# Seven quadrant products for the last six K blocks of the down projection

## The chip, the cores and the metric

The kernel runs on one core of one Trainium2 chip. The metric is the device time of one execution in microseconds (us). Its engines are PE (matrix multiplication), DVE (VectorE), ACT (ScalarE), POOL (GpSimd) and SP (SyncE, which issues the transfers here). Each engine works through its own list of instructions in order and waits on semaphores for the others.

## The reference

One layer of a streaming encoder over 544 tokens (512 of a prompt, 32 of a sample) and 1024 columns, in float32. The change concerns its last steps alone:

```
x = x + mo
x = x + swiglu(rmsnorm(x), w_gate, w_up, w_down)   # (silu(xn @ w_gate) * (xn @ w_up)) @ w_down
y = rmsnorm(x) * norm_final                        # after the only layer
```

w_gate and w_up are 1024 x 2816, w_down is 2816 x 1024: its K dimension has 22 blocks of 128 rows, its output 8 blocks of 128 columns.

## The kernel before

**Exact products.** Each float32 operand is split into a high part and a low part (ACT writes the high part, a cast to float32r; DVE writes the rest, a subtraction). One product of a 128 x 128 weight block with 272 tokens then is three matmuls: high x high, high x low, low x high. The 544 tokens are two halves of 272.

**Units of seven products.** Most of the work is cut into 2 x 2 quadrants (two output blocks, two groups of K blocks) and done by a Strassen scheme: seven products take the place of eight. In one unit PE runs `seven(q, s)`: products f = 0 to 6, each over KQ = 4 K blocks, 12 matmuls each, 84 in all. The weights of a unit come in one transfer of 1 MB into one of the two slots of `w_raw`. DVE makes three rows of sums of the quadrants (`w_sums`, line 1750 and 1754), ACT casts raw quadrants and sums into `w_hi` (its `form`, line 1124), DVE subtracts into `w_lo` (its `form`, line 1764). While PE runs unit q, ACT and DVE make the forms of unit q + 1. `form` 5 reads the last raw quadrants of a slot; SP starts the next transfer into that slot when DVE has finished it. On the way ACT copies four partial results out of PSUM (`copy_part`, line 1135, after f = 0, 1, 2 and 4), and PE waits for the copies of f = 0, 1, 2 and 4 before f = 2, 3, 4 and 6.

**The order of the feed-forward units.** `FFN` lists 30 units n = 0 to 29 in three groups c = 0, 1, 2 of 4, 4 and 3 pairs (`PAIRS`): a gate unit and an up unit for each pair of hidden blocks, and after the first gate unit of c = 1 and of c = 2 four down units, which take the eight hidden blocks of the group before. For these, each pair of hidden blocks is split in seven forms (`h_first`, `h_second`, `h_sums`, `h_sum2`, `h_sum4` on ACT, their `low_` counterparts on DVE); this happens beside the next gate unit. In c = 2 the pairs are only split plainly (`h_high` on ACT, `h_low` on DVE, line 2064).

**The tail.** The last six K blocks (NF2) of w_down belong to c = 2 and are done plainly, one output block at a time (phase "down", `unit`, `product_half`): 8 blocks x 2 halves x 6 K blocks x 3 = 288 matmuls, the last block in parts of 256 and 288 tokens. After each block DVE adds it to `resid` in `x_last`, ACT squares it (`y_sq`), POOL sums the squares (`y_sum`), PE transposes the block of the time before (`turn_y`, five transposes) and DVE writes it times `norm_final` to `y_tok`. The last block is followed by the norm of its tokens in two parts (`last_sums`, `last_norm`), the scaling of `y_tok` and six stores.

Of the kernel before, what the change touches and what calls it, by code (L numbers as in the profile page):

```python
# [39 lines left out]
    "down": (4, 2, 1),  # L40
# [106 lines left out]
def trunk_kernel(nc, x_t, cols, w_in, w_quads, ln_g, ln_b, w_s, b_s, w_pa, w_pb, w_o, w_gate, w_up, w_down_quads, w_down, norm_final,  # L147
# [30 lines left out]
    with ctx:  # L178
# [31 lines left out]
        cols64, _ = sb("cols64", [P, 9 * KD])  # L210
# [89 lines left out]
        hf_lo, _ = sb("hf_lo", [P, HFORMS, KQ, HALF], F32R, at=lo_at)  # L300
        h_quads = up_sb[:].rearrange("p i (h n) -> p (i h) n", h=2)
# [107 lines left out]
        h_ready = sem("h_ready")  # L409
# [7 lines left out]
        rstd_ready = sem("rstd_ready")  # L417
        y_turned = sem("y_turned")
        y_in_tok = sem("y_in_tok")
        ysq_done = sem("ysq_done")  # L420
# [17 lines left out]

        def form_source(q, f, slot):

            kind, n, _, _ = PRODUCTS[f]
            src = w_raw[:, slot, :].rearrange("p (f n) -> p f n", f=4) if kind == "raw" else w_sums
# [10 lines left out]
        def first_free(q):  # L453

            if q < QG:
                return firsts_taken, q + 1
            kind, c, m = FFN[q - QG]
            if kind == "down":
                return firsts_taken, QG + KQ * c + m + 1
            return (gate_made if kind == "gate" else h_made), 2 * (KQ * c + m) + 2  # L460

# [7 lines left out]
        def _(sp):  # L469
# [31 lines left out]
            def load_down(p, j, s, row, blocks, q=None):  # L501
                if q is None:
                    slot_free(p, j, s)
                else:
                    sp.wait_ge(raw_loaded[s % 2], 16)
                    sp.wait_ge(form_lo, NGROUP * q + FORM_AT[5])
                dst = w_raw[:, s % 2, 0:blocks * P].rearrange("p (k n) -> p k n", k=blocks)
                src = row_blocks(w_down, slice(row, row + blocks * P), 2 * j + s, P)
                sp.dma_start(dst, src).then_inc(raw_loaded[s % 2], 16)
# [93 lines left out]
            for n in range(len(FFN)):  # L603
                load_ffn(ph["ffn"], n)
            for s in range(2):
                load_down(ph["down"], 0, s, 0, NF2, q=QE - 2 + s)
            load_down(ph["down"], 1, 0, 0, NF2)
            sp.wait_ge(form_used, NPROD * QE)
            sp.dma_start(gf_all[:], norm_final.rearrange("(a d) -> a d", a=1).to_broadcast((P, D))).then_inc(gf_loaded, 16)
            load_down(ph["down"], 1, 1, 0, NF2)  # L610
            with sp.Fori(2, 4) as j:
                for s in range(2):
                    load_down(ph["down"], j, s, 0, NF2)
# [22 lines left out]
        def _(pe):  # L636
# [202 lines left out]
            def product(q, s, f, blocks, forms, there=None):  # L839
# [3 lines left out]
                for k in blocks:  # L843
# [6 lines left out]
                    last = pe.matmul(out, wlo, xhi, start=False, stop=k == KQ - 1, skip_group_check=not opens)  # L850
                last.then_inc(form_used, 1)

            def seven(q, s, first=None, behind={}, bank_b=None, forms=x_forms, h_made=None):
# [4 lines left out]
                def h_there(x, k):  # L858

                    if k == KQ - 1:  # L860
                        pe.wait_ge(hf_ready, h_made + {A11: 2, A12: 2, A22: 2, S3: 3, S1: 3, S2: 4, S4: 5}[x])

                for f in range(NPROD):
# [18 lines left out]
                    product(q, s, f, range(KQ), forms, there if first is not None else h_there if h_made is not None else None)  # L882
# [49 lines left out]
            seven(QG + 1, 1, behind={2: lambda: spread(r_diag, diag_ready, CH + 1, r_turned)}, bank_b=p.taken[1])  # L932
            for n, (kind, c, m) in enumerate(FFN):
                if n >= 2:
                    seven(QG + n, n % 2, behind={2: lambda: spread(r_diag, root_diag, CH + 1, root_turned)} if n == 4 else {},
                          forms=h_forms if kind == "down" else x_forms,
                          h_made=5 * (KQ * c + KQ - 1) if kind == "down" and m == 0 else None)

            def down_ready(k, h):
                if h == 0:  # L940
                    pe.wait_ge(h_ready, 2 * (k // 2) + 2)

            p = ph["down"]

            def down(j, s, ready=None):
                unit(p, j, s, H0, NF2, ready=ready)

            def turn_y(j, s):

                pe.wait_ge(dve_out[s], p.out_before(j, s) + 2)  # L950
                turn_tokens(ps_misc[s], x_last[:, s, :]).then_inc(y_turned, 1)

            pe.wait_ge(*first_free(QE - 2))
            pe.wait_ge(lo_ready, p.unit(0, 0))
            pair_free(p, 0, 0, 0)
            for h in range(2):
                product_half(p, 0, 0, 0, h, NF2, H0, P, down_ready, range(NF2 - 2), closes=False)
            for h in range(2):
                product_half(p, 0, 0, 0, h, NF2, H0, P, down_ready, (NF2 - 2, NF2 - 1), opens=False)
            pe.wait_ge(quad_out, 2 * QE)  # L960
            pe.wait_ge(*first_free(QE - 1))
            with pe.Fori(0, 3) as j:
                down(j, 1)
                turn_y(j, 0)
                down(j + 1, 0)
                turn_y(j, 1)
            pe.wait_ge(lo_ready, p.unit(3, 1))
            pair_free(p, 3, 1, 0)

            def last_block(part, behind):  # L970

                tokens, out = LAST[part], ps_main[:, 1, part, 0:LAST[part].stop - LAST[part].start]
                for k in range(NF2):
                    whi, wlo = w_hi[:, 1, k * P:(k + 1) * P], w_lo[:, 1, k * P:(k + 1) * P]
                    xhi, xlo = act_hi[:, H0 + k, tokens], act_lo[:, H0 + k, tokens]
                    pe.matmul(out, whi, xhi, start=(k == 0), stop=False)
                    pe.matmul(out, whi, xlo, start=False, stop=False)
                    last = pe.matmul(out, wlo, xhi, start=False, stop=(k == NF2 - 1))
                    if k in behind:
                        behind[k]()  # L980
                last.then_inc(tile_half, 1)

            def turn_last(part):

                pe.wait_ge(dve_out[1], p.out_before(3, 1) + part + 1)
                for c in LAST_CHUNKS[part]:
                    dst = ps_g[0:P, 0, c * P:(c + 1) * P] if c < CH else ps_g[0:NS, 1, 0:P]
                    last = pe.transpose(dst, x_last[:, 1, c * P:c * P + ROWS[c]], ident[:, :])
# [19 lines left out]
            last_block(0, {0: lambda: turn_y(3, 0)})  # L1008
            last_block(1, {0: rest_of_sums, 1: lambda: turn_last(0), 2: lambda: last_sums(0)})
# [4 lines left out]
        def _(act):  # L1014
# [104 lines left out]
            def form(q, s, f):  # L1119
# [4 lines left out]
                act.copy(f_hi[:, form_group(q, f), :], form_source(q, f, s)).then_inc(third_hi if f == 3 else form_hi, 1)  # L1124
# [195 lines left out]
            def h_high(j, i, n):  # L1320

                act.wait_ge(h_made, NF1 + n)
                act.copy(act_hi[:, H0 + 2 * j + i, :], up_sb[:, i, :]).then_inc(h_hi, 1)

# [30 lines left out]
            def h_first(n, m):  # L1355
                act.wait_ge(h_made, 2 * n + 2)
                act.copy(hf_hi[:, A11, m, :], up_sb[:, 0, 0:HALF]).then_inc(hf_split, 1)
# [13 lines left out]
            def down_hi(p):  # L1371

                act.wait_ge(raw_loaded[0], 16 * p.loads(0, 0))
                act.copy(w_hi[:, 0, 0:NF2 * P], w_raw[:, 0, 0:NF2 * P]).then_inc(hi_ready, 1)

            def up_free(n, f):
# [5 lines left out]
                elif kind == "down" and m == 0 and f == 2:  # L1382
                    act.wait_ge(hf_ready, 5 * KQ * (c + 1))
# [4 lines left out]
                elif kind == "up" and m and c < 2 and f == 2:  # L1388
                    act.wait_ge(hf_ready, 5 * pair)
                elif kind == "up" and m and c == 2:  # L1390
                    act.wait_ge(h_ready, 2 * m)

            def beside(n):
# [5 lines left out]
                if n == 1:  # L1399
                    return {3: lambda: silu(1, 1), 5: lambda: silu(2, 0)}  # L1400
                if kind == "up":
                    return {1: lambda: silu(2 * pair + 1, 1), 3: lambda: silu(2 * pair + 2, 0)}
                if kind == "down":
                    return {}
                if c == 2 and m:
                    return {0: lambda: h_high(m - 1, 1, 2 * m - 1), 2: lambda: h_high(m - 1, 0, 2 * m)}
# [7 lines left out]
            def seven(n, others):  # L1414
# [4 lines left out]
                for f in range(NPROD):  # L1419
# [1059 lines left out]
```

## Time and profile before

| | |
|---|---|
| three runs | 850.44, 850.85, 850.92 us; median 850.85 |
| profiled execution | 849.98 us, of which the span of the trace is 848.1 us |
| PE busy | 838.3 us, 99% of the span |
| DVE busy | 698.3 us, 82% |
| ACT busy | 448.3 us, 53% |
| granted clock of PE | 0.996 over the span |

An engine that is busy for 99% of the span sets the time; the others matter where PE would wait for them. The trace counts from the span's start.

### The profile page before, as it was taken

What the parts mean: (1) busy time and instruction counts of PE and PEld (TensorE: products, weight loads), DVE (VectorE), ACT (ScalarE), POOL (GpSimd) and SP (SyncE); (2) the same over time, 40 slices, a digit from 0 to 9 for tenths busy, and PEclk for the clock granted to TensorE, in tenths of its full rate; (3) what the DMA queues carried; (4) which work ended last, traced back from release to release, by engine and by line L of the source; (5) the groups of instructions that cost most, each with busy time, mean ns of one, the idle gap of its engine ahead of it and who ended that gap; (6) DMA issues with size and microseconds to landing.
All of it is one profiled execution on the core that took longest, in us unless ns stands there. A gap on an engine that the chain in (4) does not pass through costs nothing.

```text
span 848.1 us, 16289 instructions
## 1 busy us (share of the span) xinstructions
PE 838.3 (99%) x6654; PEld 836.6 (99%) x6654; DVE 698.3 (82%) x1094; ACT 448.3 (53%) x764; POOL 17.7 (2%) x23
## 2 busy tenths in 40 slices
PE   9999999999999999999999999999999999999996
PEld 9999999999999999999999999999999999999995
DVE  6868878789898989845568899999999999888554
ACT  8432225556565656652245786665566665466422
POOL 0000000000000000000000000000000000000031
PEclk9999999999999999999999999999999999999998
DMA  9333314132323232241542122222222232232222
GB/s 306 111 101 103 106 51 152 50 104 96 104 97 103 98 104 98 99 149 51 168 137 100 51 100 100 101 100 100 101 100 100 101 100 100 100 100 70 92 63 106
DMA packets 39495, 88.49 MB, mean 104 GB/s; under 512 B 2176, under 2 KB 28800, under 8 KB 33024
## 3 DMA queue, kind: packets, MB, share of 16 engines
q1 hardware_dynamic: 39424, 87.49, 30.6%
q8 instruction: 52, 0.85, 0.4%
q14 instruction: 19, 0.16, 0.1%
HBM read 85.10 MB, written 2.38 MB: 103 GB/s over the span
## 4 chain that ended last, share of the span: by engine, by line
PE 99%; DVE 0%; POOL 0%; issue 0%; DVEq 0%; ACT 0%; POOLq 0%
PE ps_main L848 13%; PE ps_main L849 13%; PE ps_main L850 13%; PE ps_main L653 10%; PE ps_main L651 10%; PE ps_main L652 10%; PE ps_t L848 7%; PE ps_t L849 7%; PE ps_t L850 7%; PE ps_g L794 1%; PE ps_g L696 1%; PE ps_t L678 1%; PE ps_main L708 0%; PE ps_main L707 0%; PE ps_main L706 0%; PE ps_g L678 0%
## 5 line engine op out<-in xcount | busy, mean ns | idle before, releaser
L848 PE MATMUL ps_main<-xf_hi,w_hi 128*128 128x272 f32 x756 | 218.6, 289 | 0.0
L849 PE MATMUL ps_main<-xf_lo,w_hi 128*128 128x272 f32 x756 | 218.5, 289 | 0.0
L850 PE MATMUL ps_main<-xf_hi,w_lo 128*128 128x272 f32 x756 | 218.4, 289 | 0.0
L651 PE MATMUL ps_main<-act_hi,w_hi 128*128 128x272 f32 x692 | 201.0, 290 | 0.0
L653 PE MATMUL ps_main<-act_hi,w_lo 128*128 128x272 f32 x692 | 200.0, 289 | 0.0
L652 PE MATMUL ps_main<-act_lo,w_hi 128*128 128x272 f32 x692 | 199.1, 288 | 0.0
L1764 DVE TENSOR_TENSOR w_lo<-w_sums,w_hi 128x1024 fp32r<-128x1024 f32 x150 | 129.8, 865 | 25.3 <-ACT w_hi L1124 24.5
L848 PEld LDWEIGHTS ps_main<-xf_hi,w_hi 128*128 128x128 f32 x756 | 142.4, 188 | 0.0
L850 PEld LDWEIGHTS ps_main<-xf_hi,w_lo 128*128 128x128 f32 x756 | 142.3, 188 | 0.0
L849 PEld LDWEIGHTS ps_main<-xf_lo,w_hi 128*128 128x128 f32 x756 | 142.2, 188 | 0.0
L1124 ACT CAST w_hi<-w_sums 128x1024 fp32r<-128x1024 f32 x150 | 114.0, 761 | 51.2 <-DVE w_sums L1754 30.4
L651 PEld LDWEIGHTS ps_main<-act_hi,w_hi 128*128 128x128 f32 x692 | 130.3, 188 | 0.2
L652 PEld LDWEIGHTS ps_main<-act_lo,w_hi 128*128 128x128 f32 x692 | 130.4, 188 | 0.0
L653 PEld LDWEIGHTS ps_main<-act_hi,w_lo 128*128 128x128 f32 x692 | 130.1, 188 | 0.0
L848 PE MATMUL ps_t<-xf_hi,w_hi 128*128 128x272 f32 x420 | 121.5, 289 | 0.0
L849 PE MATMUL ps_t<-xf_lo,w_hi 128*128 128x272 f32 x420 | 121.4, 289 | 0.0
L850 PE MATMUL ps_t<-xf_hi,w_lo 128*128 128x272 f32 x420 | 121.3, 289 | 0.0
L1764 DVE TENSOR_TENSOR w_lo<-w_raw,w_hi 128x512 fp32r<-128x512 f32 (+1 forms) x102 | 95.6, 938 | 5.1 <-ACT w_hi L1124 4.8
L1124 ACT CAST w_hi<-w_raw 128x512 fp32r<-128x512 f32 (+1 forms) x102 | 83.6, 819 | 16.9 <-PE ps_t L850 10.8
L848 PEld LDWEIGHTS ps_t<-xf_hi,w_hi 128*128 128x128 f32 x420 | 79.1, 188 | 0.2
L850 PEld LDWEIGHTS ps_t<-xf_hi,w_lo 128*128 128x128 f32 x420 | 79.0, 188 | 0.0
L849 PEld LDWEIGHTS ps_t<-xf_lo,w_hi 128*128 128x128 f32 x420 | 79.0, 188 | 0.0
(279 smaller groups left out, 1285.9 us busy)
## 6 DMA issues: line engine op xcount, KB each, us to landing
w_raw<-in_w_quads_dram SPq DMA_DIRECT2D x20, 1024.0 KB, 4.8
w_raw<-in_w_gate_dram SPq DMA_DIRECT2D x11, 1024.0 KB, 4.9
w_raw<-in_w_up_dram SPq DMA_DIRECT2D x11, 1024.0 KB, 4.8
w_raw<-in_w_down_quads_dram SPq DMA_DIRECT2D x8, 1024.0 KB, 4.9
w_raw<-in_w_in_dram SPq DMA_DIRECT2D x6, 1024.0 KB, 5.1
w_raw<-in_w_pa_dram SPq DMA_DIRECT2D x4, 1024.0 KB, 5.8
w_raw<-in_w_pb_dram SPq DMA_DIRECT2D x4, 1024.0 KB, 5.2
w_raw<-in_w_o_dram SPq DMA_DIRECT2D x4, 1024.0 KB, 6.8
```

Of the source, the lines that this page charges most:

```text
L651: pe.matmul(out, whi, xhi, start=(opens and k == order[0]), stop=False)
L652: pe.matmul(out, whi, xlo, start=False, stop=False)
L653: last = pe.matmul(out, wlo, xhi, start=False, stop=(closes and k == order[-1]))
L678: last = pe.transpose(dst, src[:, c * P:c * P + ROWS[c]], ident[:, :])
L696: pe.matmul(ps_g[:, 1, 0:P], ones[:, :], ones[:, :], start=True, stop=True)
L794: pe.matmul(ps_g[:, 0, c * P:(c + 1) * P], tok[:, c, group], ws_t[:, g, :], start=True, stop=True)
L848: pe.matmul(out, whi, xhi, start=opens and k == 0, stop=False, skip_group_check=not opens)
L849: pe.matmul(out, whi, xlo, start=False, stop=False, skip_group_check=not opens)
L850: last = pe.matmul(out, wlo, xhi, start=False, stop=k == KQ - 1, skip_group_check=not opens)
L1124: act.copy(f_hi[:, form_group(q, f), :], form_source(q, f, s)).then_inc(third_hi if f == 3 else form_hi, 1)
L1764: dve.tensor_tensor(f_lo[:, group, :], form_source(q, f, s), fbits(f_hi[:, group, :]), ALU.subtract).then_inc(third_lo if f == 3 else form ...
```

## The change

The tail becomes three more units of seven products, n = 30, 31 and 32 in `FFN`, each over KE = 3 K blocks a side (63 matmuls), for output blocks 0 to 5. The forms of a pair of c = 2 are made as for the other groups, with `h_first` and its low part over both halves (544 columns). Output blocks 6 and 7 stay plain column blocks of 36 matmuls ("tiles" 0 and 1): tile 0 runs ahead of unit 30, tile 1 after unit 32. Their weights (384 KB) come into slot 1 of `w_raw` by transfers of their own, `load_tile`. The norm follows the order of blocks 6, 1, 0, 3, 2, 5, 4, 7. For the blocks of places 5 and 6 of that order (5 and 4) ACT scales by `norm_final` ahead of the transposes (`y_scale`) and copies the transposed block to `y_tok` (`y_rows`).

```diff
-    return tuple(order)
+    return tuple(order + [("down", len(PAIRS) - 1, m) for m in range(3)])
...
+            def load_tile(q, t):
+
+                sp.wait_ge(raw_loaded[1], 16)
+                sp.wait_ge(form_lo, NGROUP * q + FORM_AT[5])
+                dst = tile_blocks(1).rearrange("p (k n) -> p k n", k=NF2)
+                sp.dma_start(dst, row_blocks(w_down, slice(0, NF2 * P), t, P)).then_inc(raw_loaded[1], 16)
...
+            load_end(first_end)
+            load_tile(ENDS - 1, KD - 2)
+            load_end(first_end + 1)
+            sp.wait_ge(form_used, NPROD * ENDS)
             sp.dma_start(gf_all[:], norm_final.rearrange("(a d) -> a d", a=1).to_broadcast((P, D))).then_inc(gf_loaded, 16)
...
+            load_end(first_end + 2)
+            load_tile(QE - 2, KD - 1)
...
+            def tile_ahead():
+
+                pe.wait_ge(tile_split, 1)
+                for h in range(2):
+                    tile_half_products(0, ps_g[:, h, 0:HALF], h, range(NF2 - 2), closes=False)
+                for h in range(2):
+                    tile_half_products(0, ps_g[:, h, 0:HALF], h, (NF2 - 1, NF2 - 2), opens=False)
...
+            turns = {ENDS - QG: {3: lambda: turn_y(0)}, ENDS - QG + 1: {5: lambda: turn_y(1)},
+                     ENDS - QG + 2: {2: lambda: turn_y(2), 4: lambda: turn_y(3), 5: lambda: turn_y(4)}}
...
+            pe.wait_ge(tile_split, 2)
+            tile_half_products(1, ps_main[:, 1, 0, 0:HALF], 0, range(NF2), behind={1: lambda: turn_y(5)})
+            pe.wait_ge(quad_out, 2 * QE)
+            tile_half_products(1, ps_main[:, 1, 1, 0:HALF], 1, range(NF2),
+                               behind={0: rest_of_rows, 2: lambda: turn_last(0), 3: lambda: last_sums(0)})
...
+            def tile_high(t):
+
+                act.wait_ge(raw_loaded[1], 16 * (raw_count(ENDS + 1) - 1 + 2 * t))
+                act.copy(tile_hi[t], tile_form(t, tile_hi[t])).then_inc(tile_cast, 1)
...
+                if kind == "up" and pair == NPAIR - 1:
+                    return {0: lambda: tile_high(0), 1: lambda: silu(2 * pair + 1, 1), 3: lambda: silu(2 * pair + 2, 0),
+                            5: lambda: h_second(pair, m)}
...
+                    return ({2: load_root, 4: lambda: y_squares(0)}, {0: lambda: y_squares(1), 5: lambda: y_squares(2)},
+                            {0: lambda: tile_high(1), 1: lambda: y_squares(3), 3: lambda: y_squares(4),
+                             6: lambda: end_block(5)})[m]
...
+                if q == ENDS + 1:
+                    take_y(0)
+                elif q == ENDS + 2:
+                    tile_low(1)
+                    take_y(2)
```

The first place is ACT during unit 29, the last up unit. `ps_t` is the bank whose copy follows f = 0, `part_112` that of f = 1; the cast of `w_raw` is form 0 of the next unit. Before:

```order
L1135 ACTIVATE ps_t<-ps_t 128x272 [waits form_used]
L1135 ACTIVATE part_112<-ps_main 128x272 [waits form_used,h_ready]
L1318 ACTIVATE gate_sb<-gate_sb 128x544 [waits gate_made]
L1135 ACTIVATE up_sb<-ps_t 128x272 [waits form_used,h_ready]
L1374 CAST w_hi<-w_raw 128x768 [waits raw_loaded0]
```

There the cast of a tail block came behind the copy of f = 2. With the change, between the copies of f = 0 and f = 1, now stands form 0 of unit 30, and behind it the cast of tile 0 (`hf_hi` holds it), which waits for the transfer into slot 1:

```order
L1190 ACTIVATE ps_t<-ps_t 128x272 [waits form_used]
L1179 CAST w_hi<-w_raw 128x384 [waits raw_loaded0]
L1427 CAST hf_hi<-w_raw 128x3x256 [waits raw_loaded1]
L1190 ACTIVATE part_112<-ps_main 128x272 [waits form_used]
L1373 ACTIVATE gate_sb<-gate_sb 128x544 [waits gate_made]
```

So the cast of a tail block moved ahead of the copy of f = 1, and form 0 of a further unit ahead of it.

The second place is ACT at the end of unit 32, from the copy of f = 4 on; before the change, a block was transposed straight from the `x_last` that DVE writes. With the change ACT stands between the end of a unit and the transposes of blocks 5 and 4 (`x_last` is now ACT's):

```order
L1190 ACTIVATE parts_103<-ps_main 128x272 [waits form_used]
L1435 ACTIVATE y_sq<-resid 128x544 [waits parts_taken,ysum_done,form_used]
L1440 ACTIVATE x_last<-resid,cols_61 128x544
L1435 ACTIVATE y_sq<-resid 128x544 [waits ysum_done,firsts_taken]
L1440 ACTIVATE x_last<-resid,cols_61 128x544
```

Two scalings and two squares moved here, behind the wait for all of unit 32.

On PE the transposes of block 5 stand behind six matmuls of tile 1, and wait for that scaling:

```order
L1003 MATMUL ps_main<-hf_hi,w_hi 128x272 [waits tile_split]
L1004 MATMUL ps_main<-hf_lo,w_hi 128x272
L1005 MATMUL ps_main<-hf_hi,w_lo 128x272
L1003 MATMUL ps_main<-hf_hi,w_hi 128x272
L1004 MATMUL ps_main<-hf_lo,w_hi 128x272
L1005 MATMUL ps_main<-hf_hi,w_lo 128x272
L722 MATMUL ps_g<-ident,x_last 128x128 [waits y_in_tok,y_scaled]
```

Before, the transposes behind such a block waited for DVE's `x_last` of the block before it (`dve_out0`, `dve_out1`).

## Rows read from the trace of the kernel before

**Rows 1.** The page, parts 1 and 2: busy us and share of the span, granted clock.
```profile
PE 838.3 (99%) x6654; PEld 836.6 (99%) x6654; DVE 698.3 (82%) x1094; ACT 448.3 (53%) x764; POOL 17.7 (2%) x23
PEclk9999999999999999999999999999999999999998
```

**Rows 2.** Busy time by stretch: PE, weight loads, DVE, ACT, POOL, clock, DMA.
```profile
760.00:770.00 10.00, 10.00 (x82) 10.00 (x81) 8.99 (x14) 5.88 (x12) 0.00 (x0) 1.00 0.28 88
```

**Rows 3.** Timeline of ACT, start and duration: copies of f = 0, then tail casts.
```profile
777.20 0.38 ACT L1135 ACTIVATE ps_main<-ps_main 128x272 f32<-128x272 f32 x1 [0.89 <-PE ps_main L850]
787.80 0.38 ACT L1135 ACTIVATE ps_t<-ps_t 128x272 f32<-128x272 f32 x1 [0.89 <-PE ps_t L850]
789.37 0.40 ACT L1135 ACTIVATE part<-ps_main 128x272 f32<-128x272 f32 x1 [1.19 <-PE ps_main L850]
...
826.26 0.83 ACT L1452 CAST w_hi<-w_raw 128x768 fp32r<-128x768 f32 x1 [3.69 <-PE ps_main L653]
827.00 0.65 ACT L1460 ACTIVATE y_sq<-x_last 128x544 f32<-128x544 f32 x1
```

**Rows 4.** Timeline around the start of unit 19, after a gate unit with all forms.
```profile
681.97 0.38 ACT L1135 ACTIVATE ps_t<-ps_t 128x272 f32<-128x272 f32 x1 [0.57 <-PE ps_t L850]
682.14 1.22 DVE L1764 TENSOR_TENSOR w_lo<-w_raw,w_hi 128x1024 fp32r<-128x1024 f32 x1
683.43 0.33 SPq L493 DMA_DIRECT2D w_raw<-in_w_down_quads_dram  x1
```

**Rows 5.** Timeline of DVE in that gate unit, 18.
```profile
675.33 0.69 DVE L1754 TENSOR_TENSOR w_sums<-w_sums,w_raw 128x512 f32<-128x512 f32 x1
675.94 0.44 DVE L2081 SCALAR_TENSOR_TENSOR up_sb<-gate_sb,up_sb 128x272 f32<-128x272 f32 x1
676.29 0.44 DVE L2104 TENSOR_TENSOR hf_lo<-up_sb,hf_hi 128x272 fp32r<-128x272 f32 x1
...
679.08 0.73 DVE L2111 TENSOR_TENSOR hf_lo<-gate_sb,hf_hi 128x544 fp32r<-128x544 f32 x1
679.71 0.45 DVE L1779 TENSOR_TENSOR gate_sb<-parts 128x272 f32<-128x272 f32 x1
```

**Rows 6.** SP's load into slot 1 in the same place of unit 29.
```profile
787.49 0.38 SPq L509 DMA_DIRECT2D w_raw<-in_w_down_dram  x1
```

**Rows 7.** Line 509, the loads of 384 KB: all eight, to landing.
```profile
DMA to landing us min/median/max: 3.1/3.4/3.4
```

**Rows 8.** Timeline of the tail: one transposed block, and the next.
```profile
805.74 0.71 PE L678 MATMUL ps_t<-ident,x_last 128*128 128x128 f32 x5
810.82 0.71 PE L678 MATMUL ps_g<-ident,x_last 128*128 128x128 f32 x5
...
832.01 0.69 DVE L2289 TENSOR_TENSOR y_tok<-ps_g,gf_all 128x512 f32 x1
832.62 0.27 DVE L2291 TENSOR_TENSOR y_tok<-ps_g,gf_all 32x128 f32 x1
```

**Rows 9.** Timeline at the end of PE's stream.
```profile
836.90 0.50 PE L1004 MATMUL ps_main<-ones,y_sq 128*128 128x1 f32 x4
838.41 0.29 PE L978 MATMUL ps_main<-act_hi,w_lo 128*128 128x288 f32 x1
838.46 0.16 DVE L2348 SCALAR_TENSOR_TENSOR rstd<-newton,rstd 128x2 f32<-128x2 f32 x1
838.74 0.46 DVE L2317 TENSOR_TENSOR x_last<-resid,ps_main 128x288 f32<-128x288 f32 x1
```

**Rows 10.** Busy time by stretch, columns as in rows 2: start and end.
```profile
1.70:5.80 4.10, 4.10 (x19) 4.10 (x20) 0.75 (x2) 1.96 (x4) 0.90 (x2) 1.00 0.85 241
5.90:6.80 0.90, 0.90 (x10) 0.90 (x10) 0.54 (x1) 0.22 (x1) 0.00 (x0) 1.00 1.03 322
...
840.50:842.10 1.60, 0.00 (x0) 0.00 (x0) 1.17 (x7) 0.65 (x3) 0.00 (x0) 1.00 0.86 346
842.10:843.10 1.00, 0.00 (x0) 0.00 (x0) 1.00 (x3) 0.93 (x1) 0.00 (x0) 0.51 1.00 397
```

More of the change, by code:

```diff
@@ L849, in product @@
                     pe.matmul(out, whi, xlo, start=False, stop=False, skip_group_check=not opens)
-                    last = pe.matmul(out, wlo, xhi, start=False, stop=k == KQ - 1, skip_group_check=not opens)
+                    last = pe.matmul(out, wlo, xhi, start=False, stop=k == blocks[-1], skip_group_check=not opens)
                 last.then_inc(form_used, 1)
@@ L881, in seven @@
                         pe.wait_ge(form_lo, NGROUP * q + FORM_AT[f])
-                    product(q, s, f, range(KQ), forms, there if first is not None else h_there if h_made is not None else None)
+                    product(q, s, f, range(KE if q >= ENDS else KQ), forms, there if first is not None else h_there if h_made is not None else None)
                     if f in behind:
@@ new lines, in tile_half_products @@
+            def tile_half_products(t, out, h, order, opens=True, closes=True, behind={}):
+                for kk in order:
+                    k, i = divmod(kk, 2)
+                    if t == 0 and k == KE - 1:
+                        pe.wait_ge(hf_ready, 5 * (NPAIR - 1) + 2 - i)
+                    if t == 0:
+                        at = (slice(0, P), 3 + k, KQ - 1, slice(i * P, (i + 1) * P))
+                        whi, wlo = hf_hi[at], hf_lo[at]
+                    else:
+                        at = (slice(0, P), kk, slice(KE * P, QUAD))
+                        whi, wlo = f_hi[at], f_lo[at]
+                    block = KQ * k + KQ - 1 if (i, h) == (0, 1) else KQ * ((A11, A12)[i] + (h if i else 0)) + k
+                    xhi, xlo = hf_hi_flat[:, block, :], hf_lo_flat[:, block, :]
+                    pe.matmul(out, whi, xhi, start=(opens and kk == order[0]), stop=False)
+                    pe.matmul(out, whi, xlo, start=False, stop=False)
+                    last = pe.matmul(out, wlo, xhi, start=False, stop=(closes and kk == order[-1]))
+                    if kk in behind:
+                        behind[kk]()
+                if closes:
+                    last.then_inc(tile_done, 1)
@@ L945, in down @@
[L945 to L981, printed above, removed]
+                    if QG + n == ENDS:
+                        tile_ahead()
@@ L983, in turn_last @@
+                    behind = {2: lambda: spread(r_diag, root_diag, CH + 1, root_turned)} if n == 4 else turns.get(n, {})
+                    seven(QG + n, n % 2, behind=behind, forms=h_forms if kind == "down" else x_forms,
+                          h_made=5 * (KQ * c + PAIRS[c] - 1) if kind == "down" and m == 0 else None)
             def turn_last(part):
-                pe.wait_ge(dve_out[1], p.out_before(3, 1) + part + 1)
+                pe.wait_ge(y_act, 1)
+                pe.wait_ge(last_made, part + 1)
@@ L1495, in _ @@
             last_squares(0)
+            y_rows(6)
             last_root(0)
@@ L2157, in gate @@
                 pair = KQ * c + m - 1
-                split, plain = n and (c < 2 or m == 0), m and c == 2
+                split, whole = n, pair >= KQ * 2
                 form(q, 0, 6)
@@ L2167, in gate @@
                     low_second(pair)
-                if plain:
-                    h_low(m - 1, 1, 2 * m - 1)
                 next_sums(n, 1)
-                if split:
+                if split and whole:
+                    low_first(pair)
                     h_sum2(pair)
-                if split:
+                elif split:
+                    h_sum2(pair)
                     low_first(pair)
@@ L2218, in up @@
                 scale_second(q, up_sb, gate_sb[:, 1, :], h_made)
-                if not last:
-                    next_form(n, 4)
+                next_form(n, 4)
+                if q + 1 == ENDS:
+                    end_of_pairs(n)
+                else:
                     next_form(n, 5)
```

377 lines of the change are left out of this document (200 added, 177 removed).

## The prediction

> **What bounds the kernel now.** I read the page first: PE is busy for 99% of the span at the full clock level (2.4 GHz of its two, 1.2 and 2.4), DVE for 82%, ACT for 53% [rows 1]. The reader is to see there that time is saved only by giving PE less to do, and lost wherever PE is made to wait. The table of stretches then says how much room the others have: in the last gate and up units DVE works 8.99 of 10 us and ACT 5.88 [rows 2]. The timelines give the prices. From ACT's copy behind f = 0 of unit 28 (777.20) to that of unit 29 (787.80) are 10.60 us for 84 matmuls, so 0.126 us for one of 272 columns [rows 3]. A plain block with its five transposes takes 5.08 us (805.74 to 810.82), of which 36 x 0.126 = 4.54 are the block [rows 8]; PE does not wait in it.
>
> **What is removed and added on PE.** The tail had 288 matmuls. Now there are 3 x 63 in the units and 2 x 36 in the tiles, 261. 27 fewer at 0.126 us give **-3.4 us**. The eight transposed blocks stay eight, and the halves of 272 and 272 cost what 256 and 288 did. All of it is lost again if PE waits elsewhere for as long.
>
> **More splitting in c = 2.** Each of the pairs 8 and 9 now needs eight DVE instructions beside a gate unit where it needed two. The stretch of unit 18 shows such a gate unit: 512 columns start 0.61 us apart (675.33 to 675.94), 272 columns 0.35, 544 columns 0.63 [rows 5]. So eight take 4 x 0.63 + 4 x 0.35 = 3.9 us in place of 2 x 0.63: +2.7 us on DVE per gate unit of 10.6. What hides it is DVE's slack, 1.0 in 10 us [rows 2], and the next up unit, which has no such work. I take 0 on PE, since units like 18 run so now and the profile shows PE without gap [rows 1]; without that cover it would be the excess, 1 us or more a unit. What is not free is that DVE is late: form 5 for unit 19 ends at 682.14 + 1.22 = 683.36, which is **1.39 us after** the copy of f = 0 of that unit began (681.97) [rows 4].
>
> **The load of tile 0 (the largest term).** That lateness now matters. SP may issue the load of tile 0 only when DVE has finished form 5 of unit 29. ACT casts tile 0 after f = 0 of unit 29, ahead of the copy of f = 1, and PE may not begin f = 3 before that copy. Counting from the start of ACT's copy of f = 0:
> - form 5 done: 1.39 as in unit 19, plus 0.28 (`low_first` is 544 columns now, 0.63 against 0.35), plus about 0.3 since ACT's cast before it grows from 272 to 544 columns too and `h_sum2` now waits for `low_first`: 2.0. Lowest 1.5, highest 2.3.
> - issue: 0.07 later (683.36 to 683.43 [rows 4]).
> - landing: 3.4 us, the median of the eight loads of this size, lowest 3.1 [rows 7].
> - ACT's cast of 768 columns: the next instruction starts 0.74 later (826.26 to 827.00); copy of f = 1: 0.40; PE's start 0.05 [rows 3].
> - together 2.0 + 0.07 + 3.4 + 0.74 + 0.40 + 0.05 = 6.65.
>
> PE's f = 0 ended when that copy began; its last matmul, 0.29 long, was issued 0.31 earlier, so f = 1 starts at -0.18, and f = 3 would be issued 24 matmuls later, at +2.85. **PE waits 6.65 - 2.85 = 3.8 us**; by the bounds 3.0 to 4.1. Queued behind ACT's cast are the copies of f = 1 and 2, a silu and forms, all of which unit 29 needs. Before, a load in the same place (787.49, 0.31 ahead of the copy at 787.80 [rows 6]) was not needed until the tail.
>
> On that landing the Trainium skill, "DMA: Bandwidth & Descriptors", section "Anatomy of one DMA — SWDGE (gpsimd) path", fits 2.0 us plus bytes by 436 GB/s. For 393,216 bytes an estimate by that page is 2.9 us. The trace has 3.4 for these very loads, issued by SP. By the page the wait would be 3.3 and the sum 0.5 lower; the trace decides.
>
> **The small units.** A unit of 63 matmuls takes 7.95 us, with a transposed block 8.5. DVE's part in unit 31: five forms and three sums at 384 columns a quadrant (by the slope of rows 5, 0.47 for 384 and 0.87 for 768: forms 3.15, sums 1.81 and 0.24 for its own waits), the two additions to `resid` 1.26, two partial results 0.70, two `take_y` of 0.61 + 0.20 [rows 8]: 8.8 us. That is 0.3 more than PE takes. PE's transposes wait for `take_y` of the block before. Slack from the wait above is used up by then, since `end_of_pairs` puts ten more DVE instructions ahead of unit 30. I take **+0.2** (0 to 0.8).
>
> **Block 5 behind ACT.** ACT waits for the whole of unit 32, then squares and scales block 5. From PE's last issue: 0.31 to its end, 0.56 until the scaling starts behind the square (0.65 for 544 columns, less the overlap of 0.09 that two ACT instructions show: 826.26 + 0.83 - 827.00), 0.65 for the scaling [rows 3], so 1.52. PE comes to the transposes one step of 0.126 behind that last issue and six matmuls of tile 1 later, at 0.88. **+0.7** (0.5 to 0.9); nothing hides it, as PE's list is in order.
>
> **The end.** Before, part 0 of the norm is summed (836.90) nine matmuls ahead of PE's last one, and DVE's chain ends at 838.62, just as the last block is ready for its addition (838.74) [rows 9]. Now only six matmuls stand between, 0.4 us less. DVE is in order, so the last addition waits: **+0.3** (0.2 to 0.5). From there to the stores the work is the same. POOL's and ACT's other new steps lie beside the 18 matmuls of each half of tile 1.
>
> **Sum.** -3.4 + 3.8 + 0.2 + 0.7 + 0.3 = **+1.6 us**. On the profiled execution of 849.98 us that is 851.6; this one ran 0.87 us under the median of the three runs (850.85), so on the median **852.5**. By the bounds: -3.4 + 3.0 + 0 + 0.5 + 0.2 = +0.3 to -3.4 + 4.1 + 0.8 + 0.9 + 0.5 = +2.9, that is 851.2 to 853.8. About 0.2% (1.7 us) is what a measurement of this kernel can tell from no change, so this forecast lies at the border of slower.
>
> **Rivals.**
> 1. *PE's clock falls in the wait.* At the end of the trace PE's last instruction ends by 840.5, and by 842.1 the granted clock is at the lower level (0.51) [rows 10]; the stretch before, from the end of the dense stream at 838.7 [rows 9], was thin too. A wait of 3.8 us is longer than both. At the start 19 matmul records stand in the 4.1 us from 1.7 to 5.8 and 10 in 0.9 us after that, so the slow stretch lasts some 4 us there, though the clock column shows 1.00 [rows 10]. At half pace 4 us lose 2 at most; I take 1.5. Time 852.5 + 1.5 = **854.0**. For it: the lengths. Against it: the end of the trace has 3.4 us without a dense matmul before the fall, nearly the whole wait here, so it depends on when in the wait the chip looks. The Trainium skill says the same of its direction: "TensorE: Matmul & The Clock Gate", Part 1, has the slow level as the default, to which an idle engine returns. No stretch of this trace shows an idle PE between dense matmuls.
> 2. *The load is there in time* (the other side). If form 5 ended as early as before the change (0.38 before the copy, as the issue at 787.49 shows [rows 6]) and the load took 3.1, the cast could start at 2.8, PE at 4.0, and the wait were 1.2: -3.4 + 1.2 + 0.2 + 0.7 + 0.3 = -1.0. The point from which it decides for faster is a wait under 0.5 us, which needs the load to land 2.1 after the copy. With no wait, and the others as summed, **848.7**. Against it: DVE's extra 2.7 us in unit 28, and the lateness of unit 19.
> 3. *DVE holds the small units back.* If DVE's 8.8 us set the pace in each of the units 30 to 32 and its backlog is not made up, PE waits about 0.8 more: **853.3**.
>
> **How the numbers follow.** The forecast 50%, the clock 30%, DVE 13%, the load in time 7%. The predicted time is the forecast's, 852.5 (own range 851.2 to 853.8). Slower by over 0.2% means above 852.55: nearly half of the forecast (0.22), nearly all of the clock's (0.28) and most of DVE's (0.10): 0.60. Faster means below 849.15: 0.04 of rival 2. The rest, 0.36, within 0.2%. The range, to hold 8 in 10, takes in the clock's 854.0 and a little above it, and leaves out rival 2: **851.0 to 854.4**.
>
> **What would show it.** In the profile of the change: PE idle for 3 to 4 us in unit 29 between f = 2 and f = 3, with ACT idle ahead of its cast of tile 0 (line 1427) until a DMA; a second wait of 0.7 us some six matmuls into tile 1, ended by ACT's line 1440; 0.8 to 1.1 us idle before the last transposes; 63 matmuls in 8 us in units 30 to 32, with PE waiting for `take_y` at most 0.8 in all. A clock column under 1.00 in the stretch behind the first wait decides for rival 1. The prediction is wrong if the cast of tile 0 does not hold the copy of f = 1, if DVE's form 5 is early, or if PE waits in the gate units 26 and 28.

## The result and the profile after

The change makes the kernel slower: 854.6 us median of six runs (854.41 to 855.53) against 850.42 of six runs before, a ratio of 1.0051 with a 95% interval of 1.0038 to 1.0064. That is 2.1 us above the forecast of 852.5 and 0.2 above the upper end of the range. From median to median the time rose by 4.2 us where the sum said 1.6: the kernel before took 0.4 less in these six runs than the 850.85 from which the forecast counted. The profiled execution took 854.76 us, 4.78 more than that of before.

The page after, parts 1 and 2, beside [rows 1]: PE is busy for 1.0 us less where 27 matmuls are 3.4, so some of the others became slower. Its share falls by a point, so it also waits more, and the third slice from the end of its row is no longer full.

```profile
span 853.0 us, 16223 instructions
PE 837.3 (98%) x6627; PEld 835.0 (98%) x6627; DVE 717.7 (84%) x1127; ACT 462.4 (54%) x800; POOL 15.1 (2%) x22
PE   9999999999999999999999999999999999999895
```

The waits of PE from 740 us on (engine, line, releaser, line: us in total, times, longest). Before, only the third of these kinds was there, as the line set apart at the end shows (0.55 in the timeline; the prediction's term of the end).

```profile
PE ps_main L892 <- ACT part L1190: 3.8, 1, 3.8
PE ps_g L722 <- DVE y_tok L2320: 1.7, 1, 1.7
PE ps_g L1035 <- DVE resid L2388: 0.9, 1, 0.9
PE ps_g L722 <- ACT x_last L1440: 0.7, 1, 0.7
...
PE ps_g L988 <- DVE x_last L2317: 0.5, 1, 0.5
```

**The first wait**, in unit 29. ACT's, DVE's and SP's rows of the timeline after (start, duration):

```profile
788.03 0.38 ACT L1190 ACTIVATE ps_t<-ps_t 128x272 f32<-128x272 f32 x1 [0.57 <-PE ps_t L894]
788.33 0.51 ACT L1179 CAST w_hi<-w_raw 128x384 fp32r<-128x384 f32 x1
793.65 0.83 ACT L1427 CAST hf_hi<-w_raw 128x768 fp32r<-128x768 f32 x1 [4.82 <-DMA w_raw<-in_w_down_dram]
794.39 0.39 ACT L1190 ACTIVATE part<-ps_main 128x272 f32<-128x272 f32 x1
...
788.80 1.22 DVE L1825 TENSOR_TENSOR w_lo<-w_raw,w_hi 128x1024 fp32r<-128x1024 f32 x1
...
790.09 0.38 SPq L553 DMA_DIRECT2D w_raw<-in_w_down_dram  x1
```

ACT has nothing to do for 4.82 us, because the cast of tile 0 waits for its transfer; the copy of f = 1 stands behind it. DVE's form 5 of unit 29 ended at 788.80 + 1.22 = 790.02, which is 1.99 behind ACT's copy at 788.03 (the forecast said 2.0).

**PE around that wait**, and the stretches behind it (stretch: us, then busy us of PE, weight loads, DVE, ACT, POOL, the granted clock, DMA share, GB/s):

```profile
790.73 0.29 PE L894 MATMUL ps_t<-xf_hi,w_lo 128*128 128x272 f32 x1
794.83 0.59 PE L892 MATMUL ps_main<-xf_hi,w_hi 128*128 128x272 f32 x1 [3.81 <-ACT part L1190]
795.22 0.43 PE L893 MATMUL ps_main<-xf_lo,w_hi 128*128 128x272 f32 x1
795.45 0.43 PE L894 MATMUL ps_main<-xf_hi,w_lo 128*128 128x272 f32 x1
...
798.17 0.34 PE L894 MATMUL ps_t<-xf_hi,w_lo 128*128 128x272 f32 x1
798.35 0.29 PE L892 MATMUL ps_t<-xf_hi,w_hi 128*128 128x272 f32 x1
```

```profile
792.00:794.00 2.00, 0.00 (x0) 0.00 (x0) 1.61 (x4) 0.35 (x1) 0.00 (x0) 1.00 0.42 124
794.00:796.00 2.00, 1.17 (x5) 1.17 (x6) 0.96 (x1) 2.00 (x5) 0.00 (x0) 0.71 0.00 0
796.00:798.00 2.00, 2.00 (x11) 2.00 (x11) 1.00 (x2) 0.38 (x2) 0.00 (x0) 0.50 0.66 178
798.00:800.00 2.00, 2.00 (x17) 2.00 (x17) 0.39 (x1) 0.93 (x3) 0.00 (x0) 0.93 0.52 215
```

Behind the wait matmuls start 0.23 us apart in place of 0.126, and the granted clock of 796 to 798 is 0.50, the lower level (1.2 GHz). From 794.83 to 798.17 PE issues 14 matmuls in 3.34 us, where 14 x 0.126 are 1.76: 1.6 us more. In this wait the clock column stands at 1.00 while PE is idle and falls as its matmuls begin again.

**The second wait**, in unit 31. DVE and POOL, start and duration; PE's transposes wait for DVE's second `take_y` row, at 823.77:

```profile
815.09 0.72 DVE L2364 TENSOR_TENSOR resid<-resid,parts 128x544 f32<-128x544 f32 x1
815.90 1.95 DVE L1825 TENSOR_TENSOR w_lo<-w_raw,w_hi 128x768 fp32r<-128x768 f32 x1
818.87 1.58 DVE L1810 TENSOR_TENSOR w_sums<-w_raw 128x768 f32<-128x768 f32 x1
822.29 0.96 DVE L1825 TENSOR_TENSOR w_lo<-w_sums,w_hi 128x768 fp32r<-128x768 f32 x1 [0.31 <-ACT w_hi L1179]
823.77 0.27 DVE L2320 TENSOR_TENSOR y_tok<-ps_g,gf_all 32x128 f32<-32x128 f32 x1
826.64 0.67 DVE L2318 TENSOR_TENSOR y_tok<-ps_g,gf_all 128x512 f32<-128x512 f32 x1
...
815.23 1.81 POOL L2479 TENSOR_TENSOR y_sum<-y_sum,y_sq 128x544 f32<-128x544 f32 x1 [11.94 <-ACT y_sq L1435]
818.27 1.36 POOL L2479 TENSOR_TENSOR y_sum<-y_sum,y_sq 128x544 f32<-128x544 f32 x1 [1.24 <-ACT y_sq L1435]
824.32 3.62 POOL L2479 TENSOR_TENSOR y_sum<-y_sum,y_sq 128x544 f32<-128x544 f32 x1 [4.68 <-ACT y_sq L1435]
```

The same subtraction of 768 columns takes 1.95 us at 815.90 and 0.96 at 822.29. The long one begins while POOL adds, and POOL ends at 815.23 + 1.81 = 817.04, some 0.8 before it. The sum at 818.87 takes 1.58 (0.94 at 791.18, without POOL) and overlaps POOL's addition until 819.63. Together DVE loses 1.0 + 0.63 us, of the 1.90 by which PE's transposes come late. The subtraction of 384 columns between the two (817.77), which ended as the second addition began, keeps its 0.54. The third addition, among DVE instructions without a gap, takes 3.62 itself.

**Sum of the rows**, by the distance of PE's rows less what the matmuls between them need: 3.97 for the wait (790.73 to 794.83, less 0.126), 1.6 for the slow matmuls, 1.90 for the transposes in unit 31, 0.84 for those of block 5, 0.31 more than before at the end (0.86 idle against 0.55), less 27 x 0.126 = 3.4: +5.2. From ACT's copy behind f = 0 of unit 28 (777.20 before [rows 3], 777.44 after) to the last addition (838.74 before, 844.33 after) the profiles differ by 5.35, so the rows leave 0.1. Ahead of that copy the profile after is 0.24 later, as it is at 600 us already. Behind the last addition, up to the end of the span, it is 0.7 shorter: 8.67 us (844.33 to 853.0) against 9.36 (838.74 to 848.1 [rows 9]), a difference that comes behind the last scaling, in the stores. 5.35 + 0.24 - 0.69 are the 4.9 between the two spans. The eleven profiles of kernels with the change have 8.65 to 8.74 us there; why the stores end sooner is not shown.

### The profile page after: what moved, and what is told of

Read it like the earlier page. It is cut to its first block, busy times and chain, and to the rows that moved or that the text cites. A ratio compares the mean times of both kernels' runs of the same rounds, so it can differ in the third digit from the quotient of the medians.

```text
span 853.0 us, 16223 instructions
## 1 busy us (share of the span) xinstructions
PE 837.3 (98%) x6627; PEld 835.0 (98%) x6627; DVE 717.7 (84%) x1127; ACT 462.4 (54%) x800; POOL 15.1 (2%) x22
## 4 chain that ended last, share of the span: by engine, by line
PE 91%; DVE 5%; issue 1%; ACT 1%; DMA 0%; POOL 0%; DVEq 0%; ACTq 0%; POOLq 0%; SPq 0%
PE ps_main L892 13%; PE ps_main L893 13%; PE ps_main L894 13%; PE ps_main L697 9%; PE ps_main L695 9%; PE ps_main L696 9%; PE ps_t L892 7%; PE ps_t L893 7%; PE ps_t L894 7%; DVE w_lo L1825 2%; PE ps_g L838 1%; DVE w_sums L1810 1%; PE ps_g L740 1%; PE ps_g L722 1%; ACT w_hi L1179 1%
## 5 line engine op out<-in xcount | busy, mean ns | idle before, releaser
L695 PE MATMUL ps_main<-act_hi,w_hi 128*128 128x272 f32 x608 | 176.5, 290 | 0.0
L697 PE MATMUL ps_main<-act_hi,w_lo 128*128 128x272 f32 x608 | 175.6, 289 | 0.0
L696 PE MATMUL ps_main<-act_lo,w_hi 128*128 128x272 f32 x608 | 175.0, 288 | 0.0
L1825 DVE TENSOR_TENSOR w_lo<-w_sums,w_hi 128x1024 fp32r<-128x1024 f32 (+1 forms) x159 | 136.1, 856 | 26.7 <-ACT w_hi L1179 25.9
L1179 ACT CAST w_hi<-w_sums 128x1024 fp32r<-128x1024 f32 (+1 forms) x159 | 119.4, 752 | 58.7 <-DVE w_sums L1814 35.8
L695 PEld LDWEIGHTS ps_main<-act_hi,w_hi 128*128 128x128 f32 x608 | 114.5, 188 | 0.1
L696 PEld LDWEIGHTS ps_main<-act_lo,w_hi 128*128 128x128 f32 x608 | 114.5, 188 | 0.0
L697 PEld LDWEIGHTS ps_main<-act_hi,w_lo 128*128 128x128 f32 x608 | 114.3, 188 | 0.0
L1825 DVE TENSOR_TENSOR w_lo<-w_raw,w_hi 128x512 fp32r<-128x512 f32 (+2 forms) x108 | 100.9, 935 | 4.9 <-ACT w_hi L1179 4.5
L1179 ACT CAST w_hi<-w_raw 128x512 fp32r<-128x512 f32 (+2 forms) x108 | 87.5, 810 | 16.5 <-PE ps_t L894 11.2
```

The costliest lines, as they stand in the source:

```text
L695: pe.matmul(out, whi, xhi, start=(opens and k == order[0]), stop=False)
L697: last = pe.matmul(out, wlo, xhi, start=False, stop=(closes and k == order[-1]))
L1179: act.copy(f_hi[:, form_group(q, f), 0:width(q)], form_source(q, f, s)).then_inc(third_hi if f == 3 else form_hi, 1)
L1825: dve.tensor_tensor(f_lo[:, group, w], form_source(q, f, s), fbits(f_hi[:, group, w]), ALU.subtract).then_inc(third_lo if f == 3 else form ...
```

## The experiments

Theory 1 is that three things add up: ACT's cast in unit 29 holds PE, the clock falls in that wait, and POOL's additions shut DVE out in unit 31. Its rivals are that DVE, fuller by 19 us than before, is the bound whatever the order, and that the slow matmuls have another cause than the idle time.

**The cast of tile 0 later** (`cast_f2`).

```diff
-   return {0: lambda: tile_high(0), 1: lambda: silu(2 * pair + 1, 1), 3: ...
+   return {1: lambda: silu(2 * pair + 1, 1), 2: lambda: tile_high(0), 3: ...
...
+               next_form(n, 2)
                if q + 1 == ENDS:
                    tile_low(0)
-               next_form(n, 2)
```

> The cast of tile 0 stands behind the copy of f = 2 of unit 29 (DVE's low part of the tile behind form 2 of unit 30), so it holds neither the copy of f = 1 nor of f = 2. Theory 1: the wait of 3.8 us ahead of f = 3 and the fall of the clock behind it (15 matmuls 0.1 us longer each, 1.5 us) come from that place alone; both go, and the time is 5.3 us under that of the change, about 849.3 us. Rival: DVE, which idles for some 4.9 us between 793.6 and 802.6 in the change, cannot give all of that back; PE then waits 1 to 3 us at the start of unit 30 for the low parts of h, and the time is 850.5 to 852.5.

Measured: 850.45 us (ten runs, ratio 1.0000, 0.9990 to 1.0009); the profiled execution took 850.29, 4.47 under that of the change. The wait for the copy is not among PE's waits any more, and the clock stays up:

```profile
796.00:798.00 2.00, 2.00 (x18) 2.00 (x17) 1.79 (x4) 1.29 (x3) 0.49 (x1) 1.00 0.57 104
```

Of the 5.3 us expected, 0.8 is missing in the profiled execution and 1.1 in the medians. The trace shows small waits in other places, 1.0 us together: 0.17 ahead of f = 6 (795.37 to 795.67, less 0.126), 0.31 in tile 0 for a low part of h, 0.22 in unit 30, and a slower start of 0.1 behind each. So theory 1 holds for its first two parts. The rival's wait for the low parts of h came too, much shorter than its 1 to 3 us. The wait for `y_tok` is still there at 1.75 us, so it doesn't come from the first one.

**The cast one step later only** (`cast_f1`): the same edit with index 1, behind the silu.

> The cast stands behind the copy of f = 1, so it holds the copy of f = 2 and PE waits ahead of f = 4, 1.5 us of work later: 3.8 - 1.5 = 2.3 us. If the clock falls in a wait of this length too, the matmuls behind it cost 0.23 us each for some 3.5 us as in the change, and the time is about 854.6 - 1.5 = 853.1 us. If it doesn't, the granted clock stays at 1.00 and the time is 854.6 - 1.5 - 1.5 = 851.6 us.

Measured: 853.36 us (six runs). PE waits 2.15 us ahead of f = 4 and the clock falls again:

```profile
795.00 0.39 PE L892 MATMUL ps_t<-xf_hi,w_hi 128*128 128x272 f32 x1 [2.15 <-ACT up_sb L1190]
795.23 0.29 PE L893 MATMUL ps_t<-xf_lo,w_hi 128*128 128x272 f32 x1
795.36 0.33 PE L894 MATMUL ps_t<-xf_hi,w_lo 128*128 128x272 f32 x1
795.49 0.43 PE L892 MATMUL ps_t<-xf_hi,w_hi 128*128 128x272 f32 x1
```

Here the first matmuls behind the wait still run at the full level, and the granted clock falls half a microsecond after PE has begun again (0.80 from 795.40 to 795.50, 0.50 behind that). Five of the six runs took 853.15 to 853.81 at a mean clock of 0.995; one took 851.37 at 0.997. That one is the time forecast without a fall (851.6), but the profile is that of another run (853.40), so that the clock stayed up there is argued from the mean alone.

**PE kept busy in the wait** (`busy_wait`): 28 matmuls whose result nobody reads.

```diff
                    if f == 3:
+                       if q == ENDS - 1:
+                           pe.wait_ge(form_lo, NGROUP * q + FORM_AT[f])
+                           for i in range(7):
+                               for k in range(KQ):
+                                   pe.matmul(ps_g[:, 0, 0:HALF], f_hi[:, f, k * P:(k + 1) * P], ...
                        pe.wait_ge(part_copied, 4 * q + 2)
```

> The change with 28 more matmuls of 272 columns on PE ahead of its wait for the copy of f = 1 in unit 29, into a PSUM bank that nobody reads then (ps_g); they add work and compute nothing that is used. They take 28 x 0.126 = 3.5 us of the 3.8 that PE waits. Theory 1: the fall of the clock comes from the idle time alone, so the clock stays at 1.00, the matmuls behind the wait start 0.126 apart, and the time falls by 1.5 us to about 853.1, although PE does more. Rival: the slow matmuls behind the wait have another cause (the transfer, ACT's burst of work); then they stay 0.227 apart and the time stays at 854.6.

Measured: 853.25 us median of six runs, 1.35 under the change (ratio to before 1.0032, 1.0020 to 1.0044). Counted from ACT's copy of f = 0, the transfer, ACT's cast and the end of the wait stand where they stood within 0.1 us (PE goes on 6.73 behind it, 6.80 in the change). What is different is the work on PE and, behind it, the distance of the matmuls and the clock:

```profile
791.36 3.67 PE L921 MATMUL ps_g<-xf_hi,w_hi 128*128 128x272 f32 x28
795.26 0.39 PE L892 MATMUL ps_main<-xf_hi,w_hi 128*128 128x272 f32 x1 [0.24 <-ACT part L1196]
795.49 0.29 PE L893 MATMUL ps_main<-xf_lo,w_hi 128*128 128x272 f32 x1
...
796.00:798.00 2.00, 2.00 (x18) 2.00 (x17) 1.21 (x2) 1.42 (x3) 0.00 (x0) 1.00 0.40 98
```

That the idle time brings the clock down, and that this costs some 1.5 us, is thereby shown: the transfer and ACT's burst are still there, and the clock stays up.

**POOL's first additions made thin** (`thin_pool`): one column in place of 544 for the first three.

```diff
-   pool.tensor_tensor(y_sum[:], y_sum[:], y_sq[:, t % 2, :], ALU.add).then_inc(ysum_done, 1)
+   w = 1 if t < 3 else N
+   pool.tensor_tensor(y_sum[:, 0:w], y_sum[:, 0:w], y_sq[:, t % 2, 0:w], ALU.add).then_inc(ysum_done, 1)
```

> POOL's first three additions of squares (blocks 6, 1 and 0) take one column in place of 544, with the same semaphores; what is left out is those three blocks' squares in the norm. Theory 1: POOL's additions hold up DVE (form of 768 columns 1.95 us beside POOL, 0.95 without; sums 1.58, 0.95 without), and these 1.6 us are the wait of 1.7 us for y_tok in unit 32. The wait falls to 0.1 to 0.3 and the time to about 853.0 us. Rival: DVE's own 8.8 us of work a unit makes the wait; then DVE's instructions keep their lengths, the wait stays over 1 us and the time moves by less than 0.5 us.

Measured: 853.88 us median of four runs (853.18 to 854.68; ratio 1.0043, 1.0027 to 1.0060), a gain of 0.7 that the runs' spread hardly tells from nothing; the profiled execution took 853.18, 1.58 under that of the change. The trace is plain: the wait for `y_tok` (in unit 31, which the expectation calls 32) is no longer in the list, 0.26 us by the distance of PE's rows against 1.90, and DVE's two rows have their usual length.

```profile
815.96 0.96 DVE L1825 TENSOR_TENSOR w_lo<-w_raw,w_hi 128x768 fp32r<-128x768 f32 x1
817.94 0.95 DVE L1810 TENSOR_TENSOR w_sums<-w_raw 128x768 f32<-128x768 f32 x1
```

**POOL's first two additions made twice** (`pool_twice`), each repeated behind itself.

```diff
+               for i in range(2 if t < 2 else 1):
+                   last = pool.tensor_tensor(y_sum[:], y_sum[:], y_sq[:, t % 2, :], ALU.add)
...
```

> The change with POOL's additions of the squares of blocks 6 and 1 made twice each (those two blocks' squares count double in the norm, which is what is computed differently). Theory 1: an addition of POOL shuts DVE's instructions with two operands in SBUF out for its 1.35 us; two more of them, where DVE has no idle time, make the wait for y_tok in unit 32 longer by 1.35 to 2.7 us, from 1.7 to 3.0 to 4.4, and the time 855.9 to 857.3 us. Rival: DVE is merely slow there for its own reasons, POOL's additions lie beside it; then the wait stays at 1.7 and the time at 854.6.

Measured: 859.11 us (ratio 1.0098, 1.0083 to 1.0114), 1.8 more than the most that was expected. The wait is 3.97 us, as theory 1 has it, and two DVE rows of 384 columns that took 0.54 now take 1.7. But in this wait the clock comes down a second time, which I had left out of the expectation. Here it falls while PE is still idle: from 824 to 826 its mean is 0.75, and of these 2 us PE works the last 0.08.

```profile
PE ps_g L723 <- DVE y_tok L2321: 4.0, 1, 4.0
...
817.27 1.72 DVE L1826 TENSOR_TENSOR w_lo<-w_sums,w_hi 128x384 fp32r<-128x384 f32 x1
820.96 1.70 DVE L1826 TENSOR_TENSOR w_lo<-w_raw,w_hi 128x384 fp32r<-128x384 f32 x1
...
824.00:826.00 2.00, 0.08 (x1) 0.11 (x2) 1.97 (x4) 1.98 (x4) 0.00 (x0) 0.75 0.00 0
828.00:830.00 2.00, 2.00 (x11) 2.00 (x11) 1.40 (x4) 0.51 (x1) 1.66 (x1) 0.50 0.00 0
```

Thin and doubled together show that POOL's additions make the wait: none listed, 1.74 and 3.97 us with the first additions thin, whole and doubled.

**The order of the end** (`end_order`).

```diff
-   ... behind={1: lambda: turn_y(5)})
+   ... behind={3: lambda: turn_y(5)})
-   behind={0: rest_of_rows, 2: lambda: turn_last(0), 3: lambda: last_sums(0)})
+   behind={0: rest_of_rows, 1: lambda: turn_last(0), 2: lambda: last_sums(0)})
```

> On PE the transposes of block 5 stand behind twelve matmuls of tile 1 in place of six, and in the last half the transposes and sums of part 0 stand one step earlier each (behind K block 1 and 2 in place of 2 and 3). Theory 1: the wait of 0.7 us for ACT's scaling goes, and the last addition comes 0.4 us or more earlier, since DVE's chain of part 0 stood ahead of it: 1.1 to 1.3 us in all, 853.4 us. Rival: ACT's copies of the transposed rows or the second scaling come late in turn, and the gain stays under 0.5 us.

Measured: 854.36 us median of four runs, which alone would not tell it from the change. The profiled execution took 853.85, 0.91 less; PE's wait for the scaling is gone and the last one is 0.62 in place of 0.86. So in the trace theory 1 holds for the wait for ACT and for about half of the end; in the medians (0.24) only the rival's figure is seen, and the gain of some 0.9 shows in `best1` below.

**Combinations.** `best1` is `cast_f2` with `end_order`. `pool_merge` is `cast_f2` with one addition of POOL in place of the first two, and block 1 squared later:

```diff
-   pool.memset(y_sum[:], 0.0).then_inc(ysum_done, 1)
-   for t in range(KD - 2):
+   pool.wait_ge(ysq_done, 2)
+   pool.tensor_tensor(y_sum[:], y_sq[:, 0, :], y_sq[:, 1, :], ALU.add).then_inc(ysum_done, 3)
+   for t in range(2, KD - 2):
...
-   {0: lambda: y_squares(1), 5: lambda: y_squares(2)}
+   {4: lambda: y_squares(1), 5: lambda: y_squares(2)}
```

> The later cast of tile 0 together with the later transposes of block 5 and the earlier end of part 0. The waits are in different places of PE's list, so the gains add up: 850.45 - 0.84 (the wait for the scaling) - 0.3 (the last wait) = 849.3. Rival: the later transposes push ACT's copies of the rows and the sums behind them, and what is won comes back before the last block: 850.0 or more.

> On top of the kernel with the later cast: POOL's first two additions (of block 6 to a cleared y_sum, of block 1 to that) become one, of the two squares to each other, and ACT squares block 1 behind the copy of f = 4 of unit 31 in place of f = 0, so that the one addition falls beside DVE's take_y, which reads PSUM. Nothing is left out. Theory 1: the two delays of DVE (1.0 and 0.63 us) shrink to 0.3 at most, the wait for y_tok falls from 1.7 to under 0.5 and the time from 850.45 to about 849.0. Rival: POOL shuts DVE out for as long in the new place (or ACT, which waits for the addition before it squares block 0, makes the forms of unit 32 late); then the time stays within 0.4 of 850.45.

> All three together: later cast, merged first addition of POOL, later transposes of block 5 and earlier end of part 0. By theory 1 all waits but some 1.5 us of small ones are gone, 849.3 - 1.5 = 847.8 us, faster than the kernel before by 2.6. Rival: the waits hide one another, and the time stays at 849 or above.

Measured: `best1` 849.57 us (0.9987, 0.9978 to 0.9996), near its 849.3. `pool_merge` 850.97, 0.5 above `cast_f2`, and `best2`, which has all three, 849.84: no gain from the merged addition, as its rival said. The first wait for `y_tok` did go (0.30 where 1.90 stood), but POOL's addition found DVE without a gap and took 3.39 us, and ACT waited for it ahead of a form and of the copy of f = 0 of unit 32, for which PE waits 1.1 us. ACT's and POOL's rows of `best2`:

```profile
817.96 0.82 ACT L1179 CAST w_hi<-w_raw 128x768 fp32r<-128x768 f32 x1
821.72 0.66 ACT L1435 ACTIVATE y_sq<-resid 128x544 f32<-128x544 f32 x1 [2.94 <-POOL y_sum L2476]
822.29 0.49 ACT L1179 CAST w_hi<-w_sums 128x384 fp32r<-128x384 f32 x1
822.69 0.38 ACT L1190 ACTIVATE ps_main<-ps_main 128x272 f32<-128x272 f32 x1
...
818.24 3.39 POOL L2476 TENSOR_TENSOR y_sum<-y_sq 128x544 f32<-128x544 f32 x1 [387.05 <-ACT y_sq L1435]
```

`best3` therefore squares block 0 behind the copy of f = 1 of unit 32, and blocks 3 and 2 behind f = 2 and 4:

```diff
-   {4: lambda: y_squares(1), 5: lambda: y_squares(2)}, {0: lambda: tile_high(1), 1: lambda: y_squares(3), 3: lambda: y_squares(4),
+   {4: lambda: y_squares(1)}, {0: lambda: tile_high(1), 1: lambda: y_squares(2), 2: lambda: y_squares(3), 4: lambda: y_squares(4),
```

> As best2, but ACT squares block 0 behind the copy of f = 1 of unit 32 in place of f = 5 of unit 31, so that it doesn't wait for POOL's addition ahead of a form and the copy of f = 0 of unit 32. Theory: the wait of 1.1 us that best2 has for that copy goes, and no other takes its place: 849.84 - 1.27 = 848.6, or 848.2 if the wait for y_tok behind it (0.5) goes too. Rival: POOL's additions, now later by one step, shut DVE out in unit 32 and make the last blocks late: 849.3 or more.

Measured: **848.03 us** (seven runs, ratio 0.9972, 0.9960 to 0.9983), faster than the kernel before by 2.5 us and than the change by 6.6. All of PE's waits from 740 us on:

```profile
PE ps_g L1035 <- DVE resid L2388: 0.6, 1, 0.6
PE ps_g L1003 <- DVE hf_lo L2167: 0.2, 1, 0.2
PE ps_g L722 <- DVE y_tok L2320: 0.2, 1, 0.2
```

Not all of the 2.5 us are PE's: behind the last addition the profile has 8.73 us (837.57 to 846.3) where before it had 9.36, so some 0.6 come from the shorter stores.

## Why the prediction was wrong

**What is saved on PE: right.** With the large waits taken away, `best3` takes 59.92 us from ACT's copy behind f = 0 of unit 28 (777.65) to the last addition (837.57), 1.62 less than before (61.54). The small waits and slow starts that its trace still shows on PE in that stretch come to some 1.65 us by the distance of its rows; together that is 3.3 of the 3.4.

**The load of tile 0: right, step for step.** Form 5 ended 1.99 behind the copy (2.0 forecast), the transfer was issued 0.07 later, the cast began 3.56 after that (3.4 to landing [rows 7]), the copy 0.74 after the cast, and PE idled 3.81 us (3.8 forecast; 3.97 by the distance of its rows).

**The clock: a step that failed.** The sum put the fall at nothing and kept it as rival 1, with 30%. It happened, and at about its price (1.6 us by the rows, 1.5 forecast). The argument that kept it below the forecast was the 3.4 us at the end of the trace before the clock fell. It doesn't hold: in `cast_f1` the clock fell behind an idle time of 2.15 us. It did not fall in or behind the 1.74 us of the second wait in the profile of the change.

**The small units: the other step that failed.** The term was +0.2 (0 to 0.8), from DVE's own 8.8 us of work a unit; it is 1.90. DVE's own work was about right: with POOL's first additions thin, 0.26 is left. Rival 3 had the right engine, but again with DVE's own work alone, and 0.8 us. What was wrong is that the count of DVE's work leaves POOL's additions out. The only words on POOL, that its steps "lie beside" the matmuls of tile 1, ask whether PE waits for it, and not whether DVE does. The sign was in the trace of before. Five of POOL's seven additions started together with a DVE subtraction and took 2.04 to 2.17 us, one started in the middle of a subtraction and took 1.57, and the one that met none took 1.35:

```profile
827.73 2.17 POOL L2409 TENSOR_TENSOR y_sum<-y_sum,y_sq 128x544 f32<-128x544 f32 x1 [2.91 <-ACT y_sq L1460]
832.66 1.35 POOL L2409 TENSOR_TENSOR y_sum<-y_sum,y_sq 128x544 f32<-128x544 f32 x1 [2.76 <-ACT y_sq L1460]
```

There POOL waited for DVE (0.94 a subtraction) and nobody waited for POOL. In the units DVE has hardly a gap to give, and the order turns: once POOL has got in, DVE waits until it is done, 1.0 and 0.63 us in the change and 1.2 for each of two rows in `pool_twice`. The Trainium skill, "SBUF — State Buffer", section "SBUF: two separate sides", says so in advance: a pair of ports is shared by DVE's instructions with two inputs in SBUF and by GpSimd's that read SBUF, as an exclusive lock; whichever starts first keeps it for its whole instruction, and the other blocks fully. This trace agrees (0.95 grows to 1.95 and 1.58 beside POOL; `take_y`, which reads PSUM, keeps its 0.67 at 826.64 in the middle of POOL's third addition). I had not weighed that rule.

**Block 5 and the end: right in size.** 0.84 against +0.7, and 0.31 against +0.3. `end_order` takes the first away. That the work from there to the stores is the same was wrong by 0.7 us, in the forecast's favour.

**The range.** It took in one of the rivals at a time. The clock and the second wait came together, 1.6 + 1.7 us over the forecast. That the time still lies near the upper end is luck: the shorter stores (0.7), which nothing in the prediction foresaw, and a kernel before that ran 0.4 lower than in the three runs the forecast counted from.

## What to carry to other kernels

Where PE is busy for 99% of the time, ask of each step that waits for a transfer what stands behind it in its engine's order; moving one cast by two places was worth 4.2 us here. Idle times of PE of 2.15, 3.81 and 3.97 us were followed here by slow matmuls worth 1.5 us or more on top, one of 1.74 us was not; so it pays to fill such a wait or to shorten it. An instruction of POOL on SBUF is not free because nobody waits for its result: look at whether DVE's neighbours grow, and in a full stretch give POOL fewer and later instructions, with nothing urgent queued behind them.

## What the runs showed that I had not expected

POOL and DVE hold each other up in both directions. An addition of 1.35 us takes 3.39 to 3.62 among DVE instructions that follow one another without a gap; DVE instructions that start after it still go ahead of it. By its end, less its 1.35 us, it gets in at the next DVE instruction that reads PSUM (826.6 in the change, 820.3 in `best2`, both at `take_y`), or about a gap of less than 0.1 us (815.81 to 815.90 in the change). PE's clock fell at three different places: as PE began again in the change, half a microsecond after that in `cast_f1`, where three matmuls ran at the full level before the slow ones, and while PE was still idle in `pool_twice`. And 28 useless matmuls made a kernel 1.35 us faster.
